# One slab of adaLN weights less in each mLSTM head, and the first output projection begun inside the last head's norm

## The chip, the core and the metric

One core of a Trainium2 chip runs the whole kernel as one launch. The metric is the time of one execution on the device, in microseconds (us), given as the median of several runs. All data are float32. Of the engines of the core, TensorE (PE in the rows) multiplies matrices, VectorE (DVE), ScalarE (ACT) and GpSimd (POOL) work elementwise, and SyncE (SP) only issues transfers.

## The reference

Two blocks follow each other on 512 latent tokens of width 1024; the first block also carries 256 context tokens. The part around the change is layer 0 of the first block:

```python
def _ada(cvec, w, b):                      # adaLN: shift, scale, gate of a layer
    m = jax.nn.silu(cvec) @ w + b
    return jnp.split(m.reshape((-1, 1, m.shape[-1])), 3, axis=-1)

h = _rms(x, norm_w[l]) * (1.0 + scale) + shift            # lat and ctx
oa = _neighbourhood_attention(qa, ka, va, k_ctx, v_ctx, rpb)   # 16 heads of 64
hb = _mlstm_bidir(lat, ctx, need_ctx)                      # 4 heads of 256, both directions

def merge(oa, hb, za, ob, zb):
    hb = hb * jax.nn.sigmoid(ob)
    hb = _rms(hb, h_norm)                  # per head
    ya = oa * jax.nn.silu(za)
    yb = hb * jax.nn.silu(zb)
    return jnp.concatenate([ya, yb], axis=-1) @ w_out      # first output projection

x = x + gate * y
```

Layer 1 is a gated linear attention (GLA) between its own adaLN, norm and output projection. The second block has an RG-LRU branch, a gated DeltaNet branch, an output projection and a gated MLP. Its part is untouched.

## The kernel before

**One list for all engines.** A Python list ORDER holds the steps of the whole kernel by name, such as ("ml_s", h, i). Each engine has a function that walks the list and emits, for the steps it takes part in, its own instructions with their semaphore waits. So where a step stands in ORDER sets its place in every engine's queue, and an engine executes its queue in that order.

**The weights' ring.** All weights arrive as slabs through a ring of three SBUF slots (NRING = 3). SyncE issues the loads in the order in which ORDER opens the slabs. Slab i goes to slot i % 3 and waits until slab i - 3 is given up, and every later load stands behind it. In an mLSTM head two slabs are used: mqk (the q and k projections) and mvo (v, and the output gate, which `ml_o` multiplies at the head's end). The adaLN weights of both layers are twelve slabs (ada0, ada1), each with two steps: `ada` (16 short matmul records, L913, then a copy of the product by VectorE into the slab, L2188) and `adat` (8 tiny ones, L921, then an addition by VectorE, L2194), which gives the slab up. The order of the slabs around mLSTM head h is mvo(h), mqk(h+1), ada, mvo(h+1).

**The neighbourhood attention** (`na_steps`) does two heads per j, j = 0 to 7, with the projection of the next j as a side list of 24 groups. The first four j have `ada` and `adat` in that side list.

**The mLSTM** (`ml_steps`). For each of four heads: scores of eight tiles (`ml_s`, L1126 on TensorE, a copy L1797 on ScalarE), values (`ml_v`, L1134, a copy L1804), and between these the norm of the head before (`ml_ya` squares on ScalarE, `ml_y` sums on TensorE L1188, `ml_yr` the reciprocal root on ScalarE L1646 and L1648, `ml_yd` four products on VectorE L2427 and L2431). Then 16 pieces: `ml_e` (VectorE argument L2365, ScalarE exp L1822), `ml_x` (VectorE product with the scores, L2374), `ml_nd` (TensorE, weighted product, L1165). `ml_o` (L1178) is the output gate's projection, four products of which two have 512 columns and two 256, with `ml_os` the sigmoid (L1854) and `ml_og` the gating (L2419). zab are the projections for the silu gates za and zb (L965).

**The first output projection** (oab) is done by a scheme with seven instead of eight block products. For each p = 0 to 3 and each segment s (0 latent, 1 context) TensorE makes the products n = 0 to 6 in four banks; they take sums of weight blocks (`sv_sums`, L2444, 1024 columns) and of activation blocks (`sv_halves`, L2454, 2048 or 1024 columns) that VectorE makes, and partial results (`sv_p1` by ScalarE, L2137, `sv_u` by VectorE, L2500 to L2517). Product 0 takes only attention outputs, product 3 only sums of them. All sums for p = 0 are made in `sv_begin`, after the last head's norm. The x of p is added, squared and summed for the next norm (`norm_pairs`, `nm` L939 and L942), then `norm_rest` scales the tiles (`nh`, VectorE L2228, ScalarE L1698) and `zc` (L951) multiplies them.

Of the kernel before, what the change touches and what calls it, by code (L numbers as in the profile page):

```python
# [44 lines left out]
SIZE = {"ada0": 4096, "ada1": 4096, "zab": 1024, "na": 3072, "gate": 1024, "mqk": 4096, "mvo": 4096,  # L45
# [3 lines left out]
CUT = (["ada0"] * 6 + ["zab"] * 16 + ["na"] * 8 + ["gate"] + ["mqk", "mvo"] * 4 + ["oab"] * 4  # L49
# [79 lines left out]
def na_side(j):  # L129
# [100 lines left out]
def ml_steps():  # L230
# [3 lines left out]
    for h in range(4):  # L234
# [9 lines left out]
        made += [("ml_os", h, 0, 1), ("ml_og", h, 0, 0), ("ml_o", h, 1, 0), ("ml_os", h, 1, 0), ("ml_og", h, 0, 1)]  # L244
        made += [("ml_o", h, 1, 1), ("ml_os", h, 1, 1), ("ml_og", h, 1, 0), ("ml_og", h, 1, 1), ("tables",)]
    for group in ml_norm(3):
        made += group + (ada.pop(0) if ada else [])
    return made
# [138 lines left out]
def norm_pairs(n, name, begun=()):  # L387
# [6 lines left out]
    return made + [("nx", n, s, 6) for s in parts] + [("nm", n, i, s) for i in range(2) for s in parts]  # L394
# [7 lines left out]
def gate_up_steps():  # L402

    made = [("gu", 0), ("gu_t",), ("gu_s", 1)]
    for j in range(1, 22):
# [10 lines left out]
         + [("tables",)] + [("sv_begin", "oab")] + norm_pairs(1, "oab") + norm_rest(1) + [("zc", j) for j in range(15)]  # L416
# [15 lines left out]
def order_of(engine):  # L432
# [6 lines left out]
    "ada": lambda l, s: [f"ada{l}"], "zab": lambda j, s, c: ["zab"] * (c == s == 0),  # L439
    "na_p": lambda j, i, s, c: ["na"] * (i == s == c == 0), "ml_gate": lambda: ["gate"],  # L440
    "ml_p": lambda h, i, s, c: ["mqk"] * (i == s == c == 0), "ml_v": lambda h, i: ["mvo"] * (i == 4),
    "oab": lambda p: ["oab"], "zc": lambda j: ["zc3" if j == 12 else "zc"] * (j % 4 == 0), "zc_": lambda c: ["zc1"] * (c == 0),
# [110 lines left out]
class Count:  # L553


    def take(self, *a, **k):
        return self
# [15 lines left out]
def build(nc, D, out):  # L573
    st = ExitStack()
    with st:
# [246 lines left out]
        SV_T = {"oab": [3072, 9216], "oc7": [3072], "wo": [1024]}  # L822
# [13 lines left out]
        def sv_t(name, s, n, k0, k1):  # L836
# [4 lines left out]
            a = SV_T[name][s] + m * w * (0, 1, 0, 2)[n]  # L841
# [26 lines left out]
        def tensor(e):  # L868
# [34 lines left out]
            def ada_ring(l, s):  # L903
                return 7 if (0, 4) <= (l, s) <= (1, 1) else proj
# [51 lines left out]
            def zab(j, s, c):  # L956
                a, b = BOTH[s]
                if c == 0:
                    if s == 0:
                        slab("zab", 8)  # L960
# [2408 lines left out]
```

## Time and profile before

| | |
|---|---|
| median of 3 runs | 3801.75 us (3801.16 to 3806.63) |
| the profiled execution's own time | 3805.69 us |
| its span, first to last instruction | 3803.9 us |
| TensorE busy | 3662.1 us, 96% of the span |
| VectorE, ScalarE, GpSimd busy | 1794.0, 1286.0, 873.3 us |
| mean granted TensorE clock | 0.990 of full speed |
| DMA queues busy | 15.6% of 16 engines |

The profile is one execution, so its times are summed and compared with its own 3805.69 us. Times of windows and timelines are counted from the span's start. The granted clock is given as a share of 2.4 GHz; the engine's other level is 1.2 GHz. A time in brackets behind a row is how long the engine sat idle before the row's first instruction, with what released it.

### The profile page before, as it was taken

Reading aid. Unit: us, or ns where it says so; the run is one execution under the profiler, and the core shown is the slowest. Engines: PE = TensorE matmul, PEld = TensorE weight load, DVE = VectorE, ACT = ScalarE, POOL = GpSimd, SP = SyncE. Lnnn points to the kernel's source line nnn. Section 1 sums busy time; section 2 is a strip of 40 time slices with the busy share of each in tenths; the row PEclk is TensorE's granted clock in tenths of the full one; section 3 lists DMA queues with packets and bytes.
Section 4 is the critical chain, followed back from the end, with each engine's and each line's share of the span. In section 5 each row is a group of like instructions: output and inputs, shape, how many; then the busy total and the mean of one; then the engine's idle time right before and its main releaser. Section 6 shows DMA issues by size and latency. Waiting matters only on the chain.

```text
span 3803.9 us, 53855 instructions
## 1 busy us (share of the span) xinstructions
PE 3662.1 (96%) x22426; PEld 2348.6 (62%) x22426; DVE 1794.0 (47%) x3209; ACT 1286.0 (34%) x2394; POOL 873.3 (23%) x888
## 2 busy tenths in 40 slices
PE   6999999999998999999999999999999999999998
PEld 3555655655555965666677776544455554478887
DVE  1433332223224320777777775355577751164543
ACT  3434443222223021444444441476454431010000
POOL 0000000001000000666666662023344531000000
PEclk9999999999999999999999999999999999999999
DMA  5111002010102111111111011121101111222221
GB/s 209 56 64 72 31 23 89 23 67 1 67 34 89 45 61 67 46 46 45 46 45 46 29 46 59 61 87 60 71 18 46 43 43 61 100 89 89 82 76 53
DMA packets 24258, 226.62 MB, mean 60 GB/s; under 512 B 2640, under 2 KB 5200, under 8 KB 8784
## 3 DMA queue, kind: packets, MB, share of 16 engines
q1 hardware_dynamic: 24016, 223.18, 15.6%
q8 instruction: 178, 2.92, 0.3%
q14 instruction: 64, 0.52, 0.0%
HBM read 221.07 MB, written 2.10 MB: 59 GB/s over the span
## 4 chain that ended last, share of the span: by engine, by line
PE 90%; DVE 5%; DMA 1%; ACT 1%; issue 1%; POOL 1%; DVEq 0%; SPq 0%; POOLq 0%; ACTq 0%
PE bank L1277 9%; PE bank L1594 7%; PE bank L1221 6%; PE bank L1287 5%; PE bank L1012 4%; PE bank L1109 4%; PE bank L965 4%; PE bank L1621 3%; PE bank L1400 3%; PE bank L1267 3%; PE bank L951 3%; PE bank L1134 2%; PE bank L1031 2%; PE bank L1539 2%; PE bank L1178 2%; PE bank L1165 2%
## 5 line engine op out<-in xcount | busy, mean ns | idle before, releaser
L1277 PE MATMUL bank<-hT,ring 128*128 128x256 f32 (+1 forms) x1024 | 349.9, 491 | 0.0
L1277 PEld LDWEIGHTS bank<-hT,ring 128*128 128x128 f32 x1024 | 190.1, 190 | 121.6 <-issue 107.9
L1012 PE MATMUL bank<-hT,ring 128*128 128x256 f32 (+1 forms) x512 | 186.3, 501 | 2.4 <-ACT hT L1698 2.4
L1400 PE MATMUL bank<-hT,ring 128*128 128x512 f32 x384 | 178.9, 600 | 4.7 <-ACT Y L1704 4.7
L965 PE MATMUL bank<-hT,ring 128*128 128x256 f32 (+1 forms) x512 | 182.3, 494 | 0.0
L1287 PE MATMUL bank<-ring,hT 128*128 128x128 f32 x1536 | 182.1, 277 | 0.0
L1287 PEld LDWEIGHTS bank<-ring,hT 128*128 128x128 f32 x1536 | 176.3, 192 | 2.0
L1109 PE MATMUL bank<-hT,ring 128*128 128x256 f32 (+1 forms) x512 | 171.8, 487 | 0.0
L1944 ACT ACTIVATE arena<-arena 128x1024 f32<-128x1024 f32 x112 | 118.2, 1055 | 100.0 <-POOL arena L3056 57.7
L3151 POOL TENSOR_TENSOR hT<-hT,arena 128x512 f32<-128x512 f32 x3 | 5.1, 1725 | 569.3 <-ACT arena L1648 569.3
L1109 PEld LDWEIGHTS bank<-hT,ring 128*128 128x128 f32 x512 | 96.6, 191 | 62.6 <-issue 53.5
L3000 POOL TENSOR_TENSOR arena<-arena,cons 128x192 f32<-128x192 f32 (+1 forms) x48 | 34.2, 750 | 423.9 <-DVE arena L2266 364.7
L1012 PEld LDWEIGHTS bank<-hT,ring 128*128 128x128 f32 x512 | 92.9, 193 | 58.3 <-issue 52.0
L965 PEld LDWEIGHTS bank<-hT,ring 128*128 128x128 f32 x512 | 91.8, 190 | 51.3 <-issue 44.5
L3068 POOL TENSOR_TENSOR arena<-arena 128x256 f32<-128x256 f32 x112 | 121.4, 1084 | 0.0
L2626 DVE TENSOR_TENSOR arena<-arena 128x256 f32<-128x256 f32 x112 | 121.2, 1082 | 0.0
L1267 PE MATMUL bank<-hT,ring 128*128 128x512 f32 x256 | 120.2, 604 | 0.0
L2633 DVE TENSOR_TENSOR arena<-arena 128x512 f32<-128x512 f32 x112 | 119.0, 1062 | 0.0
L1682 ACT ACTIVATE arena<-xT 128x512 f32<-128x512 f32 (+1 forms) x40 | 23.0, 585 | 274.6 <-DVE xT L2962 98.2
L3016 POOL TENSOR_TENSOR arena<-arena,cons 128x128 f32<-128x128 f32 x48 | 30.8, 642 | 362.3 <-DVE arena L2374 362.3
L1400 PEld LDWEIGHTS bank<-hT,ring 128*128 128x128 f32 x384 | 68.2, 190 | 73.6 <-issue 72.8
L1594 PE MATMUL bank<-arena 128*128 128x256 f32 x504 | 112.2, 380 | 0.0
(495 smaller groups left out, 7738.4 us busy)
## 6 DMA issues: line engine op xcount, KB each, us to landing
ring<-in_w SPq DMA_DIRECT2D x60, 2048.0 KB, 8.4
ring<-in_w SPq DMA_DIRECT2D x17, 1536.0 KB, 7.1
ring<-in_w SPq DMA_DIRECT2D x20, 1280.0 KB, 5.5
ring<-in_w SPq DMA_DIRECT2D x12, 1024.0 KB, 4.8
ring<-in_w SPq DMA_DIRECT2D x8, 1408.0 KB, 5.9
ring<-in_w SPq DMA_DIRECT2D x19, 512.0 KB, 3.4
xT<-in_xT SPq DMA_DIRECT2D x1, 3072.0 KB, 12.5
out<-hT SPq DMA_DIRECT2D x8, 256.0 KB, 2.1
```

Of the source, the lines that this page charges most:

```text
L965: ins = e.matmul(m, w[:, k, :], hT[:, k, a:b], start=k == 0, stop=k == 7)
L1012: ins = e.matmul(m[:, 0:b - a], w[:, k, sl(i)], hT[:, k, a:b], start=k == 0, stop=k == 7)
L1109: ins = e.matmul(m[:, 0:b - a], w[:, k, sl(i)], hT[:, k, a:b], start=k == 0, stop=k == 7)
L1221: ins = e.matmul(o[i], left[:, k], right, start=first and k == 0, stop=k == m - 1, skip_group_check=True)
L1267: ins = e.matmul(m, w[:, k, sl(0)], hT[:, k, 0:LAT], start=k == 0, stop=k == 7)
L1277: ins = e.matmul(m[:, 0:b - a], w[:, k, sl(1 + d)], hT[:, k, a:b], start=k == 0, stop=k == 7)
L1287: ins = e.matmul(m[:, sl(i % 4)], hT[:, k, a:b], w[:, k, sl(3)], start=k == 0, stop=k == 7)
L1400: ins = e.matmul(m, w[:, k, sl(i)], hT[:, k, 0:LAT], start=k == 0, stop=k == 7)
L1594: ins = e.matmul(m, l[:, k], r[:, k], start=first and k == 0, stop=k == 3, skip_group_check=True)
L2626: e.tensor_tensor(dq[:, :, lo], bk[:, :, lo], rb, ALU.subtract).then_inc(up("gl_dq", (j, li)), 1)
L2633: e.tensor_tensor(o, gl_D[(7 * j + li) % 2][:, 0:512], gl_q_[j % 2], ALU.mult).then_inc(up("gl_ql", (j, li)), 1)
L3068: e.tensor_tensor(kl[:, :, hi], dk[:, :, hi], kb[:, :, hi], ALU.mult).then_inc(up("gl_kl", (j, li)), 1)
```

## The change

Four things are edited.

1. The adaLN slabs of layer 1 number 2, 3 and 4 move from the ends of mLSTM heads 0, 1 and 2 into j = 4, 5 and 6 of the attention, where the earlier ones already stand for j = 0 to 3. The last one, (1, 5), moves from the last head's norm behind the projection: its first half (`ada_a`) stands ahead of the norm's sums `nm`, its second half behind them, `adat` behind `zc` 1.
2. The last two zab slabs become one of 2048 columns, zab2.
3. In every head two `ml_e` and an `ml_x` move from behind `ml_s` 6 to behind `ml_s` 3.
4. In the last head the `ml_o` products go (0,0), (1,0), (0,1), (1,1). A part of VectorE's sums (`oab_t`) moves ahead of the second gating, another (`oab_u`) ahead of the norm's second part, and products 0 and 3 of p = 0, both segments (`oab_`), stand between the parts of the norm; ScalarE's copies of them (`oab_p`) follow. The regions for the sums are placed anew (SV_T).

```diff
-CUT = (["ada0"] * 6 + ["zab"] * 16 + ["na"] * 8 + ["gate"] + ["mqk", "mvo"] * 4 + ["oab"] * 4
+CUT = (["ada0"] * 6 + ["zab"] * 14 + ["zab2"] + ["na"] * 8 + ["gate"] + ["mqk", "mvo"] * 4 + ["oab"] * 4
@@ na_side(j)
-    if j < 4:
-        l, s = [(0, 4), (0, 5), (1, 0), (1, 1)][j]
-        made[19].append(("ada", l, s))
-        made[21].append(("adat", l, s))
+    l, s = divmod(4 + j, 6)
+    made[19].append(("ada", l, s))
+    made[21].append(("adat", l, s))
@@ ml_steps()
             made += [(name, h, i)] + (side.pop(0) if side else [])
-        made += [("ml_e", h, *ML_PIECES[0]), ("ml_e", h, *ML_PIECES[1]), ("ml_x", h, *ML_PIECES[0])]
+            if (name, i) == ("ml_s", 3):
+                made += [("ml_e", h, *ML_PIECES[0]), ("ml_e", h, *ML_PIECES[1]), ("ml_x", h, *ML_PIECES[0])]
         attend, late = ml_attend(h)
-        ada = [[("ada", 1, 2 + h)], [("adat", 1, 2 + h)]]
-        made += attend + (ada.pop(0) if h < 3 else []) + [("ml_o", h, 0, 0)] + late + [("ml_os", h, 0, 0), ("ml_o", h, 0, 1)]
-        made += ada.pop(0) if h < 3 else []
...
-    for group in ml_norm(3):
-        made += group + (ada.pop(0) if ada else [])
-    return made
+    made += [("ml_os", 3, 0, 0), ("ml_o", 3, 1, 0), ("ml_og", 3, 0, 0), ("oab_t",), ("ml_os", 3, 1, 0), ("ml_og", 3, 1, 0),
+             ("ml_o", 3, 0, 1), ("ml_os", 3, 0, 1), ("ml_ya", 3, 0), ("ml_o", 3, 1, 1), ("ml_og", 3, 0, 1),
+             ("ml_os", 3, 1, 1), ("ml_og", 3, 1, 1), ("tables",),
+             ("ml_y", 3, 0), ("oab_", 1, 0), ("ml_yr", 3, 0), ("ml_ya", 3, 1), ("ml_yd", 3, 0), ("oab_", 1, 3), ("oab_", 0, 0),
+             ("ml_y", 3, 1), ("ml_yr", 3, 1), ("oab_", 0, 3), ("oab_u",), ("ml_yd", 3, 1)]
+    return made + [("oab_p", 1), ("oab_p", 0)]
@@ norm_pairs and its call for the second norm
-    return made + [("nx", n, s, 6) for s in parts] + [("nm", n, i, s) for i in range(2) for s in parts]
+    made += [("nx", n, s, 6) for s in parts] + list(mid)
+    return made + [("nm", n, i, s) for i in range(2) for s in parts] + list(end)
...
-         + [("tables",)] + [("sv_begin", "oab")] + norm_pairs(1, "oab") + norm_rest(1) + [("zc", j) for j in range(15)]
+         + [("tables",)] + [("sv_begin", "oab")] + norm_pairs(1, "oab", mid=[("ada_a", 1, 5)], end=[("ada", 1, 5)]) + norm_rest(1)
+         + [("zc", 0), ("zc", 1), ("adat", 1, 5)] + [("zc", j) for j in range(2, 15)]
@@ tensor engine: the early products
+            def oab_(s, n):
+                if s == 1 and n == 0:
+                    sv_open("oab", 0)
+                sv_bank("oab", 0, s, 0 if n == 0 else 2)
+                sv_product("oab", 0, s, n)
@@ vector engine: the sums in three parts
                 if name == "oab":
-                    q.wait_ge(*on("na_y", (7, 1)))
                     q.wait_ge(*on("ml_out", (3, 1, 1)))
+                    sv_halves(name, 0, 2)
+                    sv_sums(name, p, 2)
+                    sv_halves(name, 0, 3)
+                    sv_sums(name, p, 3)
+                    for n in (1, 2, 3):
+                        sv_halves(name, 1, n)
+                    return
...
+            def oab_t():
+                q.wait_ge(*on("na_y", (7, 1)))
+                q.wait_ge(*on("ml_nd", (3, 1, 1, 1)))
+                sv_sums("oab", 0, 0)
+                sv_halves("oab", 0, 0)
+                sv_halves("oab", 1, 0)
+                sv_sums("oab", 0, 1)
+
+            def oab_u():
+                q.wait_ge(*on("ml_out", (3, 0, 1)))
+                sv_halves("oab", 0, 1)
```

The lists of instructions show where this puts things. First ScalarE, at the start of mLSTM head 1, from the last two score copies (`ml_s` 2 and 3) on. Before:

```order
L1797 ACTIVATE arena<-bank 128x512 x2
L1804 ACTIVATE arena<-bank 128x256
L1797 ACTIVATE arena<-bank 128x512
L1822 ACTIVATE arena<-arena 128x512 x3
L1804 ACTIVATE arena<-bank 128x256
L1822 ACTIVATE arena<-arena 128x384
```

and of the change, where the same lines are L1832 (score copy), L1839 (value copy) and L1857 (exp):

```order
L1832 ACTIVATE arena<-bank 128x512 x2
L1857 ACTIVATE arena<-arena 128x512 x2
L1839 ACTIVATE arena<-bank 128x256
L1832 ACTIVATE arena<-bank 128x512
L1857 ACTIVATE arena<-arena 128x512
L1839 ACTIVATE arena<-bank 128x256
```

Two of the exps now stand ahead of the copies of value tile 0 and of score `ml_s` 6, instead of behind both.

Next TensorE at the end of the last mLSTM head, from its output gate's projection on. Before (L913 and L921 are `ada` and `adat` of (1, 5), L1188 the norm's sums, L1221 the projection):

```order
L913 MATMUL bank<-ring,small 32x512 x8
L1188 MATMUL bank<-Y,cons 128x512 x2
L921 MATMUL bank<-small,ring 128x2 x4
L1188 MATMUL bank<-Y,cons 128x256 x2
L1221 MATMUL bank<-Y,ring 128x256 x16
L1221 MATMUL bank<-arena 128x256 x8
L1221 MATMUL bank<-Y 128x256 x8
```

and of the change (L1202 the norm's sums, L1238 the projection):

```order
L1192 MATMUL bank<-hT,ring 128x256 x16
L1202 MATMUL bank<-Y,cons 128x512 x2
L1238 MATMUL bank<-Y,ring 128x128 x8
L1238 MATMUL bank<-arena 128x128 x8
L1238 MATMUL bank<-Y,ring 128x256 x8
L1202 MATMUL bank<-Y,cons 128x256 x2
L1238 MATMUL bank<-arena 128x256 x8
L1238 MATMUL bank<-Y,ring 128x256 x8
L1238 MATMUL bank<-arena 128x256 x8
```

Three of the early products now stand between the two parts of the norm and one behind its second part, and the adaLN products are gone from here. A row counts a float32 product once; the timeline shows two matmul records for it.

Last VectorE at the end of the second norm. Before (L2211 the norm's additions, L2228 `nh`):

```order
L2481 SCALAR_TENSOR_TENSOR xT<-hT,small,xT 128x128
L2211 TENSOR_TENSOR arena<-arena 128x512
L2211 TENSOR_TENSOR arena<-arena 128x256
L2228 SCALAR_TENSOR_TENSOR arena<-xT,small,arena 128x512 x8
L2228 SCALAR_TENSOR_TENSOR arena<-xT,small,arena 128x256 x8
```

and of the change (L2254 the additions, L2271 `nh`):

```order
L2540 SCALAR_TENSOR_TENSOR xT<-hT,small,xT 128x128
L2254 TENSOR_TENSOR arena<-arena 128x512
L2254 TENSOR_TENSOR arena<-arena 128x256
L2231 COPY ring<-bank 128x512
L2271 SCALAR_TENSOR_TENSOR arena<-xT,small,arena 128x512 x8
L2271 SCALAR_TENSOR_TENSOR arena<-xT,small,arena 128x256 x8
L2237 TENSOR_TENSOR small<-bank,cols 128x8
```

The copy of the last adaLN product now stands between the norm's additions and the first scaled tile.

## Rows read from the trace of the kernel before

**Rows 1.** Windows by stage; columns as in the first row (us).

```profile
core 0: us, PE busy (x) PEld busy (x) DVE busy (x) ACT busy (x) POOL busy (x), PEclk, DMA share, GB/s
310.44:376.40 65.96, 65.81 (x329) 38.20 (x328) 25.65 (x91) 27.17 (x74) 4.30 (x6) 1.00 0.17 60
440.31:504.23 63.92, 62.91 (x304) 36.87 (x304) 25.01 (x89) 27.17 (x74) 4.29 (x6) 1.00 0.05 17
823.47:959.21 135.74, 129.48 (x446) 79.40 (x445) 43.21 (x86) 34.12 (x71) 12.34 (x16) 0.97 0.12 47
959.21:1095.41 136.20, 130.76 (x446) 80.47 (x445) 42.86 (x84) 34.12 (x71) 12.32 (x16) 0.96 0.12 47
1095.41:1202.85 107.44, 102.10 (x349) 64.26 (x347) 33.26 (x70) 36.34 (x67) 7.71 (x12) 0.98 0.08 30
1202.85:1263.31 60.46, 48.89 (x257) 39.17 (x258) 31.75 (x37) 8.61 (x15) 0.00 (x0) 0.86 0.35 140
1263.31:1373.52 110.21, 110.20 (x674) 101.49 (x672) 35.78 (x71) 6.85 (x17) 0.00 (x0) 1.00 0.16 58
```

**Rows 2.** TensorE timeline, starts of heads 1 to 3: start, us, instruction, [idle before].

```profile
833.02 5.41 PE L1134 MATMUL bank<-ring,hT 128*128 128x256 f32 x16 [4.24 <-DMA ring<-in_w]
...
856.90 2.75 PE L1165 MATMUL bank<-arena 128*128 128x512 f32 x4 [2.02 <-DVE arena L2374]
859.45 4.56 PE L1134 MATMUL bank<-ring,hT 128*128 128x256 f32 x16
...
865.56 3.62 PE L1134 MATMUL bank<-ring,hT 128*128 128x256 f32 x16
...
967.93 6.69 PE L1134 MATMUL bank<-ring,hT 128*128 128x256 f32 x16 [3.42 <-DMA ring<-in_w]
...
993.10 2.41 PE L1165 MATMUL bank<-arena 128*128 128x512 f32 x4 [2.02 <-DVE arena L2374]
995.31 4.89 PE L1134 MATMUL bank<-ring,hT 128*128 128x256 f32 x16
...
1104.00 5.24 PE L1134 MATMUL bank<-ring,hT 128*128 128x256 f32 x16 [3.29 <-DMA ring<-in_w]
```

**Rows 3.** Waits of TensorE, 719 to 1203 us: total, times, longest.

```profile
PE bank L1165 <- DVE arena L2374: 8.1, 4, 2.0
```

**Rows 4.** Timeline of ScalarE and VectorE before the first weighted product, head 1.

```profile
855.41 1.14 ACT L1822 ACTIVATE arena<-arena 128x512 f32<-128x512 f32 x2
...
856.07 0.69 DVE L2374 TENSOR_TENSOR arena<-arena 128x512 f32<-128x512 f32 x1 [11.42 <-ACT arena L1822]
```

**Rows 5.** TensorE timeline: adaLN products in a head, and attention without them.

```profile
799.98 1.92 PE L913 MATMUL bank<-ring,small 128*32 128x512 f32 x16
...
812.25 0.95 PE L921 MATMUL bank<-small,ring 128*128 128x2 f32 x8
...
476.44 0.70 PE L1056 MATMUL bank<-arena 64*128 64x256 f32 x4 [0.86 <-DVE arena L2252]
```

**Rows 6.** Timeline behind the last head's products, three engines.

```profile
1210.49 3.64 PE L913 MATMUL bank<-ring,small 128*32 128x512 f32 x16 [7.67 <-DMA ring<-in_w]
...
1214.19 0.69 DVE L2188 COPY ring<-bank 128x512 f32<-128x512 f32 x1 [10.44 <-PE bank L913]
...
1217.25 0.69 ACT L1646 ACTIVATE Y<-bank,small 128x512 f32<-128x512 f32 x1 [11.49 <-PE bank L1188]
...
1218.63 0.75 DVE L2427 SCALAR_TENSOR_TENSOR arena<-arena,cols,Y 128x512 f32<-128x512 f32 x1 [0.49 <-ACT Y L1648]
...
1228.37 2.29 DVE L2454 TENSOR_TENSOR arena<-Y,arena 128x2048 f32<-128x2048 f32 x1
...
1232.91 1.22 DVE L2444 TENSOR_TENSOR Y<-ring 128x1024 f32<-128x1024 f32 x1
```

**Rows 7.** Timeline at the second norm's end: its sums, the first scaled tile.

```profile
1377.04 2.77 PE L942 MATMUL bank<-arena,cons 128*128 128x512 f32 x4
...
1380.37 4.50 DVE L2228 SCALAR_TENSOR_TENSOR arena<-xT,small,arena 128x512 f32<-128x512 f32 x6 [4.06 <-ACT arena L1648]
```

More of the change, by code:

```diff
@@ L910, in ada_ @@
                 b = take(ada_ring(l, s), ("ada", l, s), ("ada_copied", (l, s)))
-                for k in range(8):
+                for k in range(4):
+                    g = 32 * k
+                    e.matmul(b[g:g + 32, :], scol[:, 32 * k:32 * k + 32], w[:, k, :], start=True, stop=False)
+            def ada_(l, s):
+                if (l, s) != (1, 5):
+                    ada_a(l, s)
+                w, b = ada_w[l, s][0], bank[spot["ada", l, s]]
+                for k in range(4, 8):
                     g = 32 * (k % 4)
-                    ins = e.matmul(b[g:g + 32, :], scol[:, 32 * k:32 * k + 32], w[:, k, :], start=k < 4, stop=k >= 4)
+                    ins = e.matmul(b[g:g + 32, :], scol[:, 32 * k:32 * k + 32], w[:, k, :], start=False, stop=True)
                 ins.then_inc(up("ada_mm", (l, s)), 1)
@@ L1184, in ml_y @@
                 n = BOTH[s][1] - BOTH[s][0]
-                m = take(work, ("ml_ss", h, s), ("ml_ln", (h, s)))
+                m = take(work if h < 3 else (3, 7)[s], ("ml_ss", h, s), ("ml_ln", (h, s)))
                 for i in range(2):
@@ L1196, in seven @@
+            def seven(name, p):
+                early = name == "oab" and p == 0
+                if not early:
+                    sv_open(name, p)
                 begin = p == (1 if name == "oc7" else 0)
-                for s, (a, b) in enumerate(segs):
-                    w, t = (b - a) // 2, 4 * ((p * len(segs) + s) % 2)
-                    o = [take(t + n, (name, p, s, n), ("sv_u", (name, p, s, i)))[:, 0:w] for n, i in enumerate((3, 0, 5, 4))]
-                    lo, hi = (lambda h, k: sv_half(name, s, h, k, k + 1)[:, 0, :]), (lambda h, k: sv_half(name, s, h, m + k, m + k + 1)[:, 0, :])
+                for s in range(len(SEVEN[name][1])):
+                    for i in range(4):
+                        if not early or i in (1, 3):
+                            sv_bank(name, p, s, i)
@@ L1223, in seven @@
-                        ins.then_inc(up("sv_mm", (name, p, s, n)), 1)
+                        if not early or n not in (0, 3):
+                            sv_product(name, p, s, n)
                 if name != "wo" or p % 2:
                     give("oc" if name == "oc7" else name, "sv_mm", (name, p, s, 6))
+            def oab_(s, n):
[3 more added lines that the diff above has]
+                sv_product("oab", 0, s, n)
@@ L3314, in layout @@
     W += [slab(wa[0], (512 * s, 512 * s + 512)) for s in range(6)]
-    W += [slab(wab, (a + 128 * j, a + 128 * j + 128)) for a in (3072, 8192) for j in range(8)]
+    W += [slab(wab, (a + 128 * j, a + 128 * j + 128)) for a in (3072, 8192) for j in range(8)][0:14]
+    W += [slab(wab, (8960, 9216))]
     W += [slab(wab, *[(1024 * a + 128 * j, 1024 * a + 128 * j + 128) for a in range(3)]) for j in range(8)]
```

119 lines of the change are left out of this document (66 added, 53 removed).

## The prediction

> **What bounds the kernel now.** I read the windows by stage first: TensorE is busy 65.81 of 65.96 us in an attention step with adaLN products, 62.91 of 63.92 us in one without, 129.48 of 135.74 and 130.76 of 136.20 us in the mLSTM heads, 102.10 of 107.44 us in the last head, but only 48.89 of 60.46 us from the last head's end to the end of the projection's first column block, and there the granted clock is 0.86 [rows 1]. So TensorE is the bound in all of them, and what can be won is its idle time and the time it runs at the lower of its two levels. The TensorE timeline then says where it idles. At the start of heads 1, 2 and 3 it waits 4.24, 3.42 and 3.29 us for a slab, in front of the first value product, and later 2.02 us for VectorE's L2374, in front of the first weighted product [rows 2]; this second wait comes four times, 8.1 us in all, so in head 0 too [rows 3]. At the last head's end it waits 7.67 us for a slab, and the norm and the projection's sums follow behind it [rows 6].
>
> **The slab wait at three head starts.** The slab order mvo(h), mqk(h+1), ada, mvo(h+1) puts mvo(h+1) in the slot of mvo(h), which is given up only by the head's last `ml_o`; the next head needs it 3 products later. Without ada between them it takes the slot of mqk(h), free for most of a head. The wait goes: 4.24 + 3.42 + 3.29 = 10.95 us. The 16 matmuls behind each wait took 5.41, 6.69 and 5.24 us where the same ones take 3.62 [rows 2]: 1.79 + 3.07 + 1.62 = 6.48 us at the lower level, which I also count as gone. Sum 17.4 us. What is late next: mqk(h+2) now waits for mvo(h), given up at the head's end, and is wanted only after three value products and all scores of the next head.
>
> **The wait for L2374.** In head 1 the two exps ran at 855.41 for 1.14 us, the product at 856.07 for 0.69, and TensorE began at 856.90 [rows 2, 4]. The exps stood behind two copies that wait for TensorE's last value and score products. Moved ahead of both, they follow the copy of `ml_s` 3, and TensorE still has a value product (3.45 us from start to start, the 3.62 less the overlap) and a score (1.7 us) to do, against 1.14 us of exps and 0.69 of product: hidden, with 3 us to spare. If that cover were gone the 2.02 us would be back. Gain 8.1 us, and the slow matmuls behind two of the waits: 2.75 and 2.41 us where about 1.9 is due (2048 columns, half of the 3.62 row), 4.56 and 4.89 where 3.62 is [rows 2]: 0.85 + 0.5 + 0.94 + 1.27 = 3.6. Sum 11.7 us. By the waits alone it would be 8.1, my lower end.
>
> **The adaLN products of slabs 2 to 4.** Taken out of three heads: 3 x (1.92 + 0.95) = 8.6 us [rows 5]. Put into three attention steps: a step with them takes 65.96 us, one without 63.92 [rows 1], so 3 x 2.04 = 6.1 us; the rest fills the 0.86 us that TensorE waits there for L2252 [rows 5]. Four steps already hold such a slab, and in the row of one the busy time leaves no room for a slab wait. The transfers (2 MB more per step) are covered by that step. Net gain 2.5 us; between 1.9 and 2.5, since the records overlap their neighbours a little.
>
> **The last head's end.** The stretch is 60.46 us for one column block of 14 products and the norm's two sums. Three such blocks behind it take 110.21 us, TensorE busy throughout [rows 1], so a block is 36.7 us; seven products of 256 and seven of 128 columns, so about 3.45 and 1.8 us each. The sums have 2048 + 1024 columns, 1.7 + 0.9 = 2.6 us. TensorE's work is 39.3 us, and the early products cover the chain if VectorE keeps up. I walk it from the last `ml_o`, at 0: sum 1.7, products (1,0) and (1,3) to 5.3, (0,0) to 8.7, second sum to 9.6, (0,3) to 13.1, then (0,4), (0,1), (0,2) to 23.4. ScalarE needs about 1.35 us for the root (0.69 [rows 6] and a similar exp), so VectorE starts the norm's four products at 3.5. At 0.75 us each [rows 6] and some less for the plain ones, 2.9 us, they end at 6.4. `oab_u` (2.29) ends at 8.7. The second root is there at 10.8, its products take 1.8 (half the columns), to 12.6. Then two sums of 2048 columns, two of weights and three of 1024: 2 x 2.29 + 5 x 1.2 [rows 6] less overlap, 10.4 us, to 23.0. Product 5 needs `sv_u` 1, two additions of 0.4 behind these sums and behind product 2 at 23.4, so TensorE waits about 0.9 us there, since product 3, which used to stand between, is already done. In segment 1 the same gap is 0.6. `oab_t` (5.9 us) runs on VectorE while `ml_o` still has 12 us; it delays the gating of (1,0) to about 5 us before the first square could run anyway. Block end at 39.3 + 1.5 = 40.8. Gain 60.46 - 40.8 = 19.7 us. The lower end is what leaves this place whatever VectorE does, the slab wait and the adaLN products, 7.67 + 3.64 + 0.95 = 12.3 us [rows 5, 6]; the upper is 21, no gap at all.
>
> **Slab (1,5) in the second norm.** The first half stands where TensorE waits for the norm's additions, nothing. The second half follows the sums, which end at 1377.04 + 2.77 = 1379.8 [rows 7]; half of 1.92 us [rows 5] is 1.0, or 1.9 at the lower level, and VectorE's copy takes 0.69 [rows 6]. It stands ahead of the first scaled tile, which began at 1380.37 [rows 7], and so ends at 1381.7 to 1382.6: 1.3 to 2.2 us later, and zc behind it. I take 1.7, with `adat` 0.95 inside zc: a loss of 2.7 us. This speaks against the place, and so does a rule: the Trainium skill (TensorE: Matmul & The Clock Gate, Architectural detail) says that VectorE's queue is a strict FIFO, so that the tiles can't pass the waiting copy. By it the loss stands; could they pass, it would be only the 0.95. No row of before shows this copy here.
>
> **Sum.** 17.4 + 11.7 + 2.5 + 19.7 - 2.7 = 48.6 us. Against the profiled execution's own 3805.69 us that is 3757.1. The median of before lies 3.9 us below that execution, so I say 3753. The zab2 slab and the placing of the sums' regions cost nothing: the same matmuls, and one transfer less with half a head of cover.
>
> **Rivals.**
> - *The head starts keep a wait* (chance 0.10). ScalarE has the norm of the head before in the same stretch, and with the slab early it has 5 us less for it. Then the 11.7 us stay: gain 37, 3765. For it: ScalarE works in 34.12 of 135.74 us only, which is also against it.
> - *The early products only fill time* (0.12). The norm chain and VectorE's sums, 31.75 us of VectorE work in 60.46 [rows 1], end later than I walk them, each of products 1, 2, 5 and 6 then waits, and the lower level comes back: the stage gives the lower end, 12, instead of 19.7. Gain 41, 3761.
> - *Short gaps cost clock* (0.06). After the 2.02 us waits of heads 1 and 2 matmuls ran slow [rows 2]. If the gaps of 0.9 and 0.6 us do the same, at 1.7 us each, and the norm gap too, 5 us go: 3758. The Trainium skill (the same page, HAM oscillation) has the rule that a wait between groups of matmuls can bring the next group in at half clock; the rows after the waits agree, 5.41 us where 3.62 is due. For a gap of under 1 us no row shows it.
> - *The slabs stay late* (0.03). If SyncE's queue stands behind another load, the change doesn't do what it says at the head starts: 17.4 us stay, 3770.
> - *More than forecast* (0.08): the copy in the norm is hidden, the last head's gaps are nil and the 1.5 and 2.7 us come back, with a little clock: 3747 or less.
> - *Slower* (0.02). There is one zab slab less, so every later slab sits in another slot. If each of the 16 GLA slabs then came late, at 3.29 + 1.62 = 4.9 us [rows 2], 78 us would go: 3753 + 78 = 3831. It decides from 3 us per slab. Against it: each slab still waits for the one three back, and these later three keep their order.
> - *No difference* (0.01).
>
> **The numbers.** The forecast, 45 to 52 us of gain, has the remaining 0.58, so 3750 to 3757. To hold 8 in 10 the range goes down to 3746 and up to 3766, which takes in the first two rivals nearly whole and the third. About 0.2% (7.6 us) is what a measurement of this kernel can tell from no change; faster by more 0.96, within it 0.02, slower 0.02.
>
> **What the changed profile would show.** No wait for `ring<-in_w` in front of the value products, nor for VectorE's product in front of the first weighted product; heads 1 and 2 of 123 us instead of 136; attention steps of 66 us in j = 4 to 6; from the last `ml_o` to the second column block 41 us, with TensorE busy but for one gap of about 1 us ahead of product 5; the first zc matmul about 10 us behind the projection's end, not 8.5. I am wrong if a head start still shows a wait of 2 us, or if that stretch takes over 46 us, or if GLA takes longer than before.

## The result, and the profile after

| | before | changed |
|---|---|---|
| median | 3801.68 us (3801.16 to 3806.63, 4 runs) | 3756.2 us (3755.7 to 3757.34, 4 runs) |
| profiled execution, own time | 3805.69 us | 3755.7 us |
| its mean granted clock | 0.990 | 0.994 |

The ratio is 0.9878, 95% interval 0.9861 to 0.9895: faster by 45.5 us by the medians, and by 50.0 us by the two profiled executions. The page of the changed kernel's profile gives the span and the busy time of each engine; TensorE lost 15.9 us of busy time, the others nothing:

```profile
span 3753.9 us, 53854 instructions
...
PE 3646.2 (97%) x22426; PEld 2337.6 (62%) x22426; DVE 1795.7 (48%) x3209; ACT 1285.9 (34%) x2394; POOL 873.7 (23%) x888
```

Its windows by stage, which answer to [rows 1] in the same order, with a step that has now gained a slab first, then heads 1, 2 and 3, the last head's end with the first column block, the other three blocks, and everything from the first `zc` matmul on:

```profile
core 0: us, PE busy (x) PEld busy (x) DVE busy (x) ACT busy (x) POOL busy (x), PEclk, DMA share, GB/s
414.01:479.96 65.95, 65.80 (x329) 38.13 (x328) 25.64 (x91) 27.20 (x74) 4.29 (x6) 1.00 0.18 69
826.77:949.42 122.65, 122.65 (x422) 75.97 (x421) 42.36 (x82) 34.03 (x71) 12.32 (x16) 1.00 0.09 35
949.42:1072.06 122.64, 122.64 (x421) 75.97 (x420) 42.37 (x82) 34.03 (x71) 12.32 (x16) 1.00 0.09 35
1072.06:1171.99 99.93, 99.93 (x349) 63.38 (x348) 38.88 (x74) 37.28 (x69) 7.71 (x12) 1.00 0.08 32
1171.99:1212.88 40.89, 39.76 (x233) 35.29 (x232) 25.41 (x31) 7.47 (x13) 0.00 (x0) 1.00 0.25 103
1212.88:1322.93 110.05, 110.05 (x674) 101.33 (x672) 35.40 (x71) 6.86 (x17) 0.00 (x0) 1.00 0.16 58
1331.25:3753.90 2422.65, 2352.26 (x16812) 1523.27 (x16812) 1330.21 (x1994) 862.93 (x1411) 789.25 (x769) 0.99 0.16 59
```

The heads have no idle time and no low clock left: 122.65 us busy of 122.65. The last head's end is a third shorter, at full clock. Untouched blocks kept their time (110.05 us against 110.21).

All waits of TensorE between 700 and 1215 us of the changed kernel (total, times, longest) show neither the slab wait nor the one for VectorE's product L2374 (the 0.6 us stand ahead of head 0's first instruction):

```profile
engine line waited for: us in total, times, longest us
PE bank L1238 <- DVE hT L2562: 1.1, 2, 0.7
PE bank L1140 <- ACT arena L1825: 0.6, 1, 0.6
```

To locate every microsecond I counted each kernel's stages from TensorE's timeline, from one stage's first matmul to the next one's. The last head's end and the norm are counted from the end of the matmul ahead of them, less the 0.16 us by which a following one overlaps it; so the last head's end has 60.64 us here and 60.46 in [rows 1].

| stage, us | before | changed | difference |
|---|---|---|---|
| start to the attention | 93.4 | 97.4 | +4.0 |
| attention | 528.9 | 533.4 | +4.5 |
| head 0 | 125.26 | 120.05 | -5.21 |
| head 1 | 135.74 | 122.65 | -13.09 |
| head 2 | 136.19 | 122.64 | -13.55 |
| head 3 | 107.26 | 99.94 | -7.32 |
| last `ml_o` to the end of the first column block | 60.64 | 40.88 | -19.76 |
| norm behind the projection, to `zc` | 8.67 | 8.32 | -0.35 |
| the rest | 2421.88 | 2422.65 | +0.77 |

These add up to the 50.0 us; the projections ahead of head 0 (75.9 us) and the three later blocks of the projection differ by 0.01 us at most.

### The profile page after: what moved, and what is told of

Same layout as the page of the kernel before. It is cut to its first block, busy times and chain, and to the rows that moved or that the text cites. A ratio compares the mean times of both kernels' runs of the same rounds, so it can differ in the third digit from the quotient of the medians.

```text
span 3753.9 us, 53854 instructions
## 1 busy us (share of the span) xinstructions
PE 3646.2 (97%) x22426; PEld 2337.6 (62%) x22426; DVE 1795.7 (48%) x3209; ACT 1285.9 (34%) x2394; POOL 873.7 (23%) x888
## 4 chain that ended last, share of the span: by engine, by line
PE 92%; DVE 4%; issue 1%; ACT 1%; POOL 1%; DMA 1%; DVEq 0%; SPq 0%; POOLq 0%; ACTq 0%
PE bank L1312 9%; PE bank L1238 7%; PE bank L1629 7%; PE bank L1322 5%; PE bank L1123 4%; PE bank L1026 4%; PE bank L979 4%; PE bank L1656 4%; PE bank L1435 3%; PE bank L1302 3%; PE bank L965 3%; PE bank L1045 2%; PE bank L1574 2%; PE bank L1148 2%; PE bank L1394 2%; PE bank L1192 2%
## 5 line engine op out<-in xcount | busy, mean ns | idle before, releaser
L3188 POOL TENSOR_TENSOR arena<-arena,hT 128x512 f32<-128x512 f32 x48 | 74.6, 1554 | 146.8 <-DVE arena L2851 146.8
```

## Experiments

The kernel before had medians of 3806.52, 3802.93 and 3802.41 us (7 runs each) beside the three sets of runs: the first set is the first four kernels, the third `sums_early`, `three_late` and `whole_mid`, the second the rest. Each ratio is to the one beside it.

### The first part alone: only_slabs

The kernel before with slabs (1, 2) to (1, 4) in the attention, and nothing else.

```diff
-    if j < 4:
-        l, s = [(0, 4), (0, 5), (1, 0), (1, 1)][j]
...
+    l, s = divmod(4 + j, 6)
...
@@ ml_steps()
-        made += attend + (ada.pop(0) if h < 3 else []) + [("ml_o", h, 0, 0)] + late + [("ml_os", h, 0, 0), ("ml_o", h, 0, 1)]
-        made += ada.pop(0) if h < 3 else []
+        made += attend + [("ml_o", h, 0, 0)] + late + [("ml_os", h, 0, 0), ("ml_o", h, 0, 1)]
```

> The kernel before with part 1 alone for slabs (1,2) to (1,4): they go into the attention, nothing else changes. Theory (the terms add up): the slab waits at heads 1 to 3 and the slow matmuls behind them go, 17.4 us, and 2.5 us of adaLN work net, so 3801.7 - 20 = 3782 us; the waits for L2374 (4 x 2.02 us) and the wait for slab (1,5), 7.67 us, stay as they are. Rival (the wait only moves): with values earlier the wait for the first weighted product takes over what the slab wait gave, 3795 to 3799 us, and L2374's wait is 6 us at heads 1 to 3.

3788.85 us, ratio 0.9957 (0.9943 to 0.9972), 17.7 us below the kernel before beside it (some 16 by the ratio): less than the theory's 20, more than the rival allows. The slab waits at the head starts are gone, and the wait for L2374 (here L2372) stays at 2.02 us four times. But heads 0 to 3 took 124.01, 126.59, 126.61 and 103.88 us: 23.4 us less than in the kernel before, of which the adaLN products are 8.6, so 14.8 us and not 17.4 come from the slab waits. TensorE's timeline of this kernel, in heads 0 and 1, shows why:

```profile
727.46 2.56 PE L1163 MATMUL bank<-arena 128*128 128x512 f32 x4 [2.02 <-DVE arena L2372]
729.81 4.75 PE L1132 MATMUL bank<-ring,hT 128*128 128x256 f32 x16
...
854.06 2.85 PE L1163 MATMUL bank<-arena 128*128 128x512 f32 x4 [2.02 <-DVE arena L2372]
```

The matmuls behind the remaining wait are slow now in all four heads; in the kernel before they were so in heads 1 and 2 alone [rows 2]. In the rows of before the slab waits cost 10.95 us, the slow products behind them 6.48 and three lost overlaps of 0.25 (see `exps_back`) 0.75, 18.2 in all; the two slow stretches more, 1.7 us each, give back 3.4 of them, and 14.8 are left. In head 3 a slab wait had stood ahead of this one and is gone; in head 0 none had, so that the slow products there don't follow from the edit.

### The first part undone: slabs_back

```diff
-    l, s = divmod(4 + j, 6)
...
+    if j < 4:
+        l, s = [(0, 4), (0, 5), (1, 0), (1, 1)][j]
...
-        made += attend + [("ml_o", h, 0, 0)] + late
+        made += attend + [("ada", 1, 2 + h)] * (h < 3) + [("ml_o", h, 0, 0)] + late
...
+            made += [("ml_os", h, 0, 0), ("ml_o", h, 0, 1), ("adat", 1, 2 + h), ("ml_os", h, 0, 1), ...
```

> The changed kernel with slabs (1,2) to (1,4) back in the mLSTM heads, all else as changed. Theory: slab waits of 3 to 4 us in front of the first value product return at heads 1 to 3, with slow matmuls behind them: 3756.2 + 17.4 + 2.5 = 3776 us. Rival (the parts overlap, so that the exps' new place already hides most of it): under 3766 us.

3776.03 us, ratio 0.9921 (0.9904 to 0.9937), 19.8 us above the changed kernel (some 16 by the ratios). The waits are back, and the slow products behind them; the waits of TensorE in the heads, and the timeline at head 1, of this kernel:

```profile
PE bank L1149 <- DMA ring<-in_w: 10.3, 3, 4.1
```
```profile
833.21 6.75 PE L1149 MATMUL bank<-ring,hT 128*128 128x256 f32 x16 [4.06 <-DMA ring<-in_w]
```

Its heads take 26.1 us more than those of the changed kernel (122.99, 132.95, 130.61, 104.80 us). Less the 8.6 us of adaLN products that is 17.5, the forecast's 17.4: 10.3 us of waits, and 7.2 of slow products and lost overlaps.

### The third part undone: exps_back

```diff
-            if (name, i) == ("ml_s", 3):
-                made += [("ml_e", h, *ML_PIECES[0]), ("ml_e", h, *ML_PIECES[1]), ("ml_x", h, *ML_PIECES[0])]
+        made += [("ml_e", h, *ML_PIECES[0]), ("ml_e", h, *ML_PIECES[1]), ("ml_x", h, *ML_PIECES[0])]
```

> The changed kernel with the two ml_e and the ml_x of each head back behind ml_s 6. Theory: a wait of 2.02 us in front of the first weighted product returns in four heads, 8.1 us, 3764.3 us, and if short waits alone bring the lower clock another 0 to 3.6 us, up to 3768. Rival (the wait was a follow-up of the late slab): no wait in heads 1 to 3, 3756 to 3758 us.

3772.94 us, ratio 0.9917 (0.9902 to 0.9931), 16.7 us above the changed kernel by the medians (some 15 by the ratios, since the kernel before had a higher median in this set), more than expected. Heads 0 to 3 are 2.27, 3.95, 3.96 and 3.95 us longer, 14.1 us. The same wait, in TensorE's timeline of heads 0 and 1 of this kernel:

```profile
728.03 1.96 PE L1178 MATMUL bank<-arena 128*128 128x512 f32 x4 [2.02 <-DVE arena L2416]
729.82 3.62 PE L1147 MATMUL bank<-ring,hT 128*128 128x256 f32 x16
...
852.94 3.04 PE L1178 MATMUL bank<-arena 128*128 128x512 f32 x4 [2.02 <-DVE arena L2416]
855.78 4.27 PE L1147 MATMUL bank<-ring,hT 128*128 128x256 f32 x16
```

In head 0 the wait costs 2.02 us and 0.25 more, since a group that follows a wait can't overlap the one ahead of it; in head 1 the two groups behind it take 7.31 us instead of 5.58, which is the other 1.7. The forecast had 8.1 + 3.6 us: it counted slow products behind two of the four waits, as in the trace of before, and no lost overlap.

### The fourth part undone: no_early

The changed kernel with the last head's gates, norm and sums in the order of before; (1, 5) stays behind the projection.

```diff
-    made += [("ml_os", 3, 0, 0), ("ml_o", 3, 1, 0), ("ml_og", 3, 0, 0), ("oab_t",), ("ml_os", 3, 1, 0), ("ml_og", 3, 1, 0),
...
+    for group in ml_norm(3):
+        made += group
...
```

> The changed kernel without part 4: the last head ends as before, all fourteen products of the first column block stand behind the norm, all sums are made in one go behind the norm; slab (1,5) stays in the second norm, so no slab is waited for. Theory: before, the second column block began 46.1 us after the end of the norm's first sum; that chain can now start at once, the squares being there 2.9 us after the last ml_o, so the block ends about 50 us after it, against 40.9 in the changed kernel: 3756.2 + 9 = 3765 us. Rival (the slab wait was the whole loss, the early products are worth nothing): 3756 to 3758 us. Rival 2 (the early products are worth what I gave them, 19.7 - 12.3): 3764 us, not to be told from the first by time, but by where the block ends.

3764.74 us, ratio 0.9896 (0.9881 to 0.9911). The stage from the last `ml_o` to the end of the first column block takes 50.82 us instead of 40.88. So of the 19.8 us saved there 9.8 come from taking the slab away (with the zab slabs joined, as this kernel keeps them) and 9.9 from part 4. The forecast's lower end had 12.3 for the slab, "what leaves this place whatever VectorE does"; 2.5 of these come back. Behind the slab wait the kernel before waits 1.11, 1.00, 0.47, 0.98 and 0.37 us in this stage; `no_early` waits 2.57, 1.90, 0.47, 3.01 and 0.37, 4.4 us more, and has about 2.4 us less of slow products. TensorE's timeline of `no_early` shows what part 4 removes:

```profile
1174.43 1.96 PE L1198 MATMUL bank<-Y,cons 128*128 128x512 f32 x4 [2.57 <-ACT Y L1892]
1178.28 1.10 PE L1198 MATMUL bank<-Y,cons 128*128 128x256 f32 x4 [1.90 <-ACT Y L1892]
...
1190.04 5.38 PE L1234 MATMUL bank<-arena 128*128 128x256 f32 x16 [3.01 <-DVE arena L2492]
```

Two waits for the squares, and one of 3.01 us for VectorE's sums with slow products behind it.

### Part 4 with the sums but without the early products: sums_early

```diff
-             ("ml_y", 3, 0), ("oab_", 1, 0), ("ml_yr", 3, 0), ("ml_ya", 3, 1), ("ml_yd", 3, 0), ("oab_", 1, 3), ("oab_", 0, 0),
-             ("ml_y", 3, 1), ("ml_yr", 3, 1), ("oab_", 0, 3), ("oab_u",), ("ml_yd", 3, 1)]
+             ("ml_y", 3, 0), ("ml_yr", 3, 0), ("ml_ya", 3, 1), ("ml_yd", 3, 0),
+             ("ml_y", 3, 1), ("ml_yr", 3, 1), ("oab_u",), ("ml_yd", 3, 1)]
...
```

> The changed kernel with VectorE's sums early as changed (oab_t ahead of the second gating, oab_u ahead of the norm's second part), but no early product: all fourteen stand behind the norm's second sum. It splits the 9.9 us that the early part was worth in no_early. Theory A (the early products cover the chain, as the prediction reckoned): without them TensorE idles through norm and sums, block end 46 to 51 us after the last ml_o, 3761 to 3766 us. Theory B (VectorE's sums were the chain, and their place is what counts): by the rows of the changed kernel the squares of the norm's second part are there 4 us after the last ml_o, TensorE waits 2.3 us for them, and then finds every sum ready, also without the gap ahead of product 5: block end 41.6 to 42.5 us, 3756 to 3758 us.

3757.33 us, ratio 0.9883 (0.9868 to 0.9898); the stage takes 44.44 us, between the two theories (46 to 51 and 41.6 to 42.5), nearer to B, which had the wait but not the slow products behind it. Moving the gates and VectorE's sums forward thus brings 6.4 of the 9.9 us, and the products that give the change its name 3.6, in this order of adding them. These 3.6 are in the main one wait for the squares and the slow products behind it (1.90, 0.41 and 1.39 us), in this kernel's timeline of TensorE:

```profile
1171.89 1.44 PE L1202 MATMUL bank<-Y,cons 128*128 128x256 f32 x4 [1.90 <-ACT Y L1896]
1173.13 5.01 PE L1238 MATMUL bank<-Y,ring 128*128 128x256 f32 x16
```

Theory A, that TensorE would stand idle through norm and sums without the early products, falls: in their ordinary place products 0 and 4 fill that time too. By the time alone, 3757.33 against 3756.2 us, these runs tell nothing; the stage does.

### One early product back in its place: three_late

```diff
-             ("ml_y", 3, 1), ("ml_yr", 3, 1), ("oab_", 0, 3), ("oab_u",), ("ml_yd", 3, 1)]
+             ("ml_y", 3, 1), ("ml_yr", 3, 1), ("oab_u",), ("ml_yd", 3, 1)]
...
```

> The changed kernel with product 3 of the latent segment back between products 2 and 5. Theory: the gap ahead of product 5 (0.68 us) comes of sv_u 1, which starts when product 2 has ended, and goes when product 3 stands between; but product 4 now follows the norm's second sum at once and waits 1.7 us for ScalarE's copy of product 0, which stands behind the second root. Block end 40.9 + 0.9 = 41.8 us; the whole 1 us more, too little to tell. Rival (the gap comes of VectorE's late sums): a gap ahead of product 5 stays.

3759.46 us, ratio 0.9883 (0.9867 to 0.99); the stage takes 41.91 us, 1.0 more. Both as the theory had it: the gap of 0.68 us ahead of product 5 is gone, and product 4 waits 1.71 us, since product (0, 3) doesn't cover ScalarE's copy of product 0 any more. ScalarE's and TensorE's timelines of this kernel:

```profile
1182.71 0.53 ACT L2172 ACTIVATE hT<-bank 128x128 f32<-128x128 f32 x2
...
1183.49 3.69 PE L1238 MATMUL bank<-Y,ring 128*128 128x256 f32 x16 [1.71 <-DVE arena L2470]
```

The row names VectorE's L2470 because that ended at about the same time; by the code, product 4 waits for no result of L2470, but for ScalarE's copy, which ends at 1183.24. The difference in time, 3.3 us, isn't told from none by these runs; the stage tells it.

### The two zab slabs apart: zab_two

```diff
-CUT = (["ada0"] * 6 + ["zab"] * 14 + ["zab2"] + ...
+CUT = (["ada0"] * 6 + ["zab"] * 16 + ...
...
```

> The changed kernel with the last two zab slabs apart again, as before the change. In the prediction I priced joining them at nothing. By the ring's order it is not nothing: with two slabs between mvo(3) and the first oab slab, that slab falls into the slot of mvo(3) and can be loaded only behind the last ml_o, 8 us or so; VectorE's first sums wait for it ahead of the second gating, and squares, norm and all products of the block follow. Expected by that: the first column block ends 55 to 58 us after the last ml_o instead of 40.9, 3756 + 16 = 3772 us. By the prediction's own sentence: 3756 us.

3773.94 us, ratio 0.9917 (0.99 to 0.9933), 18 us above the changed kernel. The stage is 58.15 us instead of 40.88, 17.3 more and at the top of what was expected; the heads ahead of it are as in the changed kernel, and what else differs between the attention's start and GLA is low clock, 1.7 us at the attention's first matmuls and 1.7 at those of `zc`. The timeline of VectorE and then of TensorE in this kernel:

```profile
1177.50 1.22 DVE L2487 TENSOR_TENSOR arena<-ring 128x1024 f32<-128x1024 f32 x1 [19.22 <-DMA ring<-in_w]
...
1184.61 3.75 PE L1202 MATMUL bank<-Y,cons 128*128 128x512 f32 x4 [14.69 <-ACT Y L1896]
```

One slab more ahead of it shifts every later slab by one slot: the projection's slab now takes the slot of mvo(3), given up only by the last `ml_o`. `oab_t` waits for it on VectorE; behind `oab_t` stands the second gating, behind that the squares and the norm's sum on TensorE: 14.7 us of wait, and 2.5 of slow products. The edit that looked like a detail is what makes part 4 worth having.

### The adaLN slab in the norm: copy_late, last_in_attention, whole_mid

In `copy_late` the second half of (1, 5) follows `norm_rest`, so VectorE's copy stands behind all scaled tiles. In `last_in_attention` the slab stands in j = 7 of the attention. In `whole_mid` both halves stand ahead of the sums.

```diff
...
-    mid=[("ada_a", 1, 5)], end=[("ada", 1, 5)]) + norm_rest(1)
+    mid=[("ada_a", 1, 5)]) + norm_rest(1) + [("ada", 1, 5)]       # copy_late
+    mid=[("ada_a", 1, 5), ("ada", 1, 5)]) + norm_rest(1)          # whole_mid
@@ na_side(7), for last_in_attention
+        made[19].append(("ada", 1, 5))
+        made[21].append(("adat", 1, 5))
...
```

> The changed kernel with the step of slab (1,5)'s second half behind the sixteen tile scalings in the list: TensorE's place is the same, VectorE's copy comes after the tiles. Theory (the copy stands in the way): from the projection's end to the first zc 7.65 us instead of 8.32, as in the kernel that has no adaLN product there; 0.7 us less in the whole, too little for the time to show. Rival (TensorE's own second half makes the gap longer): 8.3 us as before.

> The changed kernel with slab (1,5) in the attention's last step too, nothing of it in the second norm or zc. Theory: the attention grows by 2 to 2.9 us (the other three cost 2.04 each), the gap ahead of zc is 7.65 us instead of 8.32 and zc loses the 0.95 us of adat; all in all 0.4 to 1.3 us more, which the time can't tell. Rival (the first half in the norm's gap keeps the clock up): a stretch at the lower clock comes back between projection and zc, gap 8.7 us as before, 2 us more.

> The changed kernel with both halves of slab (1,5) ahead of the norm's last sums, and so VectorE's copy too. Theory: TensorE has the time there (it waits for the additions), the copy is done before the roots, so the gap ahead of zc is 7.65 instead of 8.32 us, and zc finds its bank free, unlike with the late copy. 0.7 us less than the changed kernel, 3755 us; the time can't tell it, the trace can. Rival: the second half delays the norm's sums by what it takes, 0.9 us, gap 8.3 or more.

All three close the norm's gap from 8.32 to 7.65 us (`only_slabs`, with nothing of the slab there, has 7.65 too), so the copy in front of the tiles costs 0.67 us. None makes a faster kernel that can be told from the changed one. `copy_late`, 3759.41 us, ratio 0.9881 (0.9866 to 0.9895), gives the gain away: `zc` needs the bank that the copy still has to empty, and from the projection's end to the first GLA product it takes 114.49 us, the changed kernel 112.35. TensorE's and VectorE's timelines of `copy_late`:

```profile
1337.24 7.13 PE L965 MATMUL bank<-hT,ring 128*128 128x512 f32 x16 [2.55 <-DVE ring L2231]
...
1336.50 0.68 DVE L2231 COPY ring<-bank 128x512 f32<-128x512 f32 x1
```

`last_in_attention`, 3759.47 us, ratio 0.9878 (0.9863 to 0.9893), pays in the attention: 537.98 us against 533.44, of which 1.6 is a stretch of low clock at 93 us and 2.9 the slab. From the projection's end to the first GLA product it takes 112.42 us: the rival's 8.7 us of gap did not come, but its stretch of low clock did, 1.7 us in the first `zc` products.

`whole_mid`, 3755.47 us, ratio 0.9879 (0.9864 to 0.9893), has neither the wait for the bank nor the longer attention, and `zc` finds its bank free. But its first 32 `zc` matmuls ran slow behind the wait for ScalarE's first tile, and the same stretch takes 113.08 us, 0.7 more than in the changed kernel. TensorE at the first `zc`, in the changed kernel and in `whole_mid`:

```profile
1331.25 13.97 PE L965 MATMUL bank<-hT,ring 128*128 128x512 f32 x32 [2.32 <-ACT hT L1733]
```
```profile
1330.77 15.38 PE L965 MATMUL bank<-hT,ring 128*128 128x512 f32 x32 [2.64 <-ACT hT L1733]
```

That the place of the second half keeps the clock up is not shown either. With it where the change has it and the same wait of 2.32 us, these 32 matmuls took 13.97 us in four profiles (the changed kernel twice, `sums_early`, `three_late`) and 15.47 to 15.67 in four others (`slabs_back`, `exps_back`, `no_early`, `zab_two`). Which of the arrangements is best stays open.

### The changed kernel once more: changed_again

> The changed kernel once more, as the reference for the three beside it, since stages that no kernel here touches differed by up to 5 us between executions of the last call. Expected: 3756 us within 3 us; the stages from the attention to the first zc as in its first trace, to 0.1 us wherever the clock is full.

3755.86 us, ratio 0.9871 (0.9856 to 0.9885). Its heads, the last head's end and the norm's gap repeat to 0.01 us (120.05, 122.65, 122.65, 99.93, 40.88, 8.32). The start differs. The windows of the first 92 us, of the changed kernel and of this one:

```profile
0.00:92.00 92.00, 65.44 (x223) 32.77 (x224) 17.22 (x30) 30.46 (x52) 9.36 (x19) 0.89 0.51 200
```
```profile
0.00:92.00 92.00, 65.64 (x239) 33.02 (x239) 17.10 (x35) 31.68 (x55) 9.29 (x19) 0.93 0.52 205
```

The same program ran at 0.89 in one and at 0.93 in the other and reached the attention at 97.4 and 93.1 us. Over all thirteen profiles this start lies between 92.5 and 97.6 us, whatever was changed behind it. The rest behind the norm took 2422.65 and 2426.30 us. So a difference of up to 5 us between two single profiles says nothing unless its stage is known.

## Why the prediction was right

It said 3753 us (3746 to 3766) and 3757.1 for a profiled execution; 3756.2 and 3755.7 were measured. The mechanisms are those that it named; that the sum agrees to 1.4 us is in part luck, as the steps show. In the order of its sum:

- **Slab waits, 17.4 us.** Right: 17.5 by `slabs_back`, with the waits and the slow products that it named. The overlap that each wait also costs, 0.25 us, was left out; the waits of `slabs_back` are 0.6 us shorter than those of before, which hides it.
- **The wait for L2374, 11.7 us.** The mechanism is right, and the size too small: 14.1 us by `exps_back`. What was mis-sized is "and the slow matmuls behind two of the waits": in `exps_back` slow products follow three of the four, and each wait costs 0.25 us of overlap besides. In the two profiles of before and after, both head terms together are 39.2 us less 8.6 of adaLN products, 30.6, where the forecast had 29.1; seven lost overlaps of 0.25 (1.75 us) cover that difference, since in the trace of before slow products did follow only two of the four.
- **adaLN slabs 2 to 4, 2.5 us.** Right: three attention steps cost 6.1 us (533.4 of attention in `changed_again` and `only_slabs`, where the kernel before had 528.94, of which 1.6 are low clock at its first matmuls), and the heads lose 8.6.
- **The last head's end, 19.7 us.** Right: 60.46 to 40.89 by the windows, 19.6, and 19.8 by the count of stages above. The walk of the changed kernel holds in its parts as well. VectorE began the norm's products 3.4 us behind the last `ml_o` (forecast 3.5), ended `oab_u` at 8.6 (8.7) and the sums at 23.0 (23.0); the gap ahead of product 5 was 0.68 us (0.9) and the one in segment 1 0.45 (0.6). What the walk didn't price is the same stage without the early products. They "cover the chain", but so would products 0 and 4 in their place: 6.4 of part 4's 9.9 us come from the earlier gates and sums. And the lower end of 12.3 us was no lower end, since without part 4 it is 9.8. TensorE's timeline of the changed kernel, and VectorE's first norm product and last sum:

```profile
1171.99 1.88 PE L1202 MATMUL bank<-Y,cons 128*128 128x512 f32 x4
1173.71 1.95 PE L1238 MATMUL bank<-Y,ring 128*128 128x128 f32 x16
...
1180.73 1.03 PE L1202 MATMUL bank<-Y,cons 128*128 128x256 f32 x4
...
1196.25 3.69 PE L1238 MATMUL bank<-arena,ring 128*128 128x256 f32 x16 [0.68 <-DVE hT L2562]
...
1209.21 2.05 PE L1238 MATMUL bank<-arena,ring 128*128 128x128 f32 x16 [0.45 <-DVE hT L2562]
...
1175.36 0.75 DVE L2470 SCALAR_TENSOR_TENSOR arena<-arena,cols,Y 128x512 f32<-128x512 f32 x1 [2.26 <-ACT Y L1683]
...
1193.73 1.22 DVE L2497 TENSOR_TENSOR arena<-Y,arena 128x1024 f32<-128x1024 f32 x1
```

- **Slab (1, 5) in the second norm, -2.7 us.** Too large: at full clock it is -1.6, of which `adat` is the 0.95 that was forecast (from the first `zc` matmul to the first of GLA, 104.03 us against 103.08) and the copy's delay 0.67. In the two profiles the gap even became 0.35 us shorter, by luck: that of before, 8.67 us, has 1.0 us of low clock in it, for the same norm takes 7.65 in `only_slabs`. With 0.77 us more behind it the two profiles show -0.4. The forecast had the first `zc` matmul about 10 us behind the projection's end; it came at 8.32. The failed step is "it stands ahead of the first scaled tile, which began at 1380.37": that start belonged to a norm whose sums ran at the lower level, 2.77 us for four matmuls [rows 7]. At full clock they take 1.45, the first tile starts 1.0 us behind their end instead of 0.56, and the copy's delay is 0.67 us rather than 1.3 to 2.2. The sum there has a slip besides: 1379.8 and 1.0 or 1.9 and 0.69 make 1381.5 to 1382.4, not 1381.7 to 1382.6. VectorE's tiles did wait behind the copy: they follow it here, and in `copy_late`, without it, the gap is 0.67 us shorter. With that the rule of the Trainium skill that I cited (TensorE: Matmul & The Clock Gate, Architectural detail) agrees; what was wrong is the time from which the delay was counted. The changed kernel's timeline (TensorE, then VectorE):

```profile
1326.48 1.45 PE L956 MATMUL bank<-arena,cons 128*128 128x512 f32 x4
...
1329.00 0.69 DVE L2231 COPY ring<-bank 128x512 f32<-128x512 f32 x1 [3.11 <-PE bank L927]
```

- **The zab2 slab "cost nothing".** Wrong as a price of the edit: without it 17 to 18 us are lost. The prediction asked what the edit costs, not what it makes possible, though the slot arithmetic that it used for the head starts answers that too. It left the sum right only because the change has the edit.
- **The starts and ends that I took as equal.** The profiled changed kernel was 2.4 us behind the one of before at the start (4.0 longer there, and 1.6 less of low clock in the attention), by chance as `changed_again` shows. The terms as measured, 30.6 + 2.5 + 19.8 - 0.4 - 2.4, give the 50 us. So the stages that the sum is about brought 52.5 us where it had 48.6, and the start's chance took 2.4 back: the agreement is better than the terms. The medians differ by 45.5, because the profiled execution of before lay 4 us above its median and the changed one didn't.

Of the rivals, the one of a wait kept at the head starts is refuted by the waits above. So is the one of late GLA slabs: behind the norm neither trace has a wait of TensorE for a slab, and from GLA's first matmul to the end it took 2318.62 us against 2318.80 (2322.27 in `changed_again`). The one of early products that only fill time is refuted as to the total. Part of it is true: two thirds of what part 4 brings come from earlier gates and sums. The two short gaps cost no clock: behind 0.68 us the group took 3.69 us, behind 0.45 2.05, each within 0.1 of its like. The prediction says of a gap of under 1 us that "no row shows it"; that was misread, for the kernel before has one ahead of the same product 5, at full clock (second row). A gap of 1.00 us soon behind its slab wait has a slow group behind it (first row), so the length alone doesn't decide:

```profile
1221.42 6.23 PE L1221 MATMUL bank<-Y,ring 128*128 128x256 f32 x16 [1.00 <-ACT Y L1646]
...
1243.19 3.69 PE L1221 MATMUL bank<-arena,ring 128*128 128x256 f32 x16 [0.98 <-DVE hT L2503]
```

The Trainium skill (TensorE: Matmul & The Clock Gate, HAM oscillation) describes groups of matmuls that start at half clock behind a wait for a transfer. Behind all waits for slabs here, 3.07 to 7.73 us in `before`, `only_slabs` and `slabs_back`, the rows agree. Behind shorter waits they are divided: the groups behind 2.57 and 1.90 us in `no_early` ran at 1.96 and 1.10 us, near the 1.88 and 1.03 of the changed kernel, the one behind 1.90 in `sums_early` slow, and the two short gaps show nothing of it.

What stays open: why one of four equal waits of 2.02 us brought no lower clock in `exps_back`, and two of four in the kernel before. The rows give one hint. In `only_slabs`, whose heads 1 to 3 start 126.6 us apart, the two groups behind the wait take 7.31 us together in every head, but split as 2.56 + 4.75, 2.85 + 4.45, 3.16 + 4.15 and 3.46 + 3.85: the slow stretch begins some 0.3 us earlier, counted from the wait, in each next head. So its place doesn't hang on the wait alone. What sets it no run here tests.

## What to carry to other kernels

With a ring of slots and a queue that loads in order, ask of every slab whose slot it takes and when that one is given up: here one slab less took away a stall of 3.3 to 4.2 us in each of three heads, and one more brought a stall of 15 us at the last head's end. Price a wait with what follows it, here 2.02 us with 0.25 of overlap and often 1.7 us of slow products, and don't expect the clock's losses to add up: with some of the waits gone, those left had it behind them more often (four and three of four, instead of two, in one profile each). Before starting late work early, see whether the work ahead of it on the other engines can go first: reordered gates and sums brought 6.4 us, the early products 3.6.

## What was not expected of the hardware

The lower clock isn't tied to one wait. The same 2.02 us wait cost 2.27 us in one head and 3.95 in the next three; in `only_slabs` it brought the lower level in heads 0 and 3, where the kernel before had none, and `exps_back` had it in head 3 and not in head 0. With all waits of the heads gone, the granted clock was 1.00 throughout them. That the times then spread less is not shown: the changed kernel's eight lie between 3754.84 and 3757.91 us and those of the kernel before between 3798.34 and 3810.03, but `whole_mid` and `three_late`, whose heads are as free of waits, range over 6 and 7 us in four executions each, and `zab_two`, with its stall of 15 us, over 1.3.
